# Up projection by seven block products, feed-forward weights in 512-column slots, down results added to the output by DMA

## What is computed

```python
u = rmsnorm(x) ; proj = u @ w_in          # 88 column tiles of 128
y_a = stick_breaking_attention(...)       # 8 heads x 128
y_b = hgrn2_chunkwise(...)                # 8 heads, rmsnorm, silu gate
m = sigmoid(gate_a) * (y_a @ p_a) + sigmoid(gate_b) * (y_b @ p_b)
h = x + m @ w_o
up = rmsnorm(h) @ w_up                    # 2048 -> 2 * 5632
up = causal_depthwise_conv(up, conv_w, conv_b)      # width 3, over tokens
gate, val = split(up)
out = h + (silu(gate) * val) @ w_down     # 5632 -> 2048
```

## Time and profile before

| | us |
|---|---|
| median of 3 runs | 2946.11 |
| lowest, highest | 2946.01, 2946.46 |
| span of the profiled execution | 2944.1 |

### The profile page before, as it was taken

The page is one execution under the profiler, slowest core; times in us unless marked ns, Lnnn a source line. Parts: engine busy times, 40 slices in busy tenths (PEclk is TensorE's granted clock), DMA queues, the critical chain, the costliest instruction groups (busy, mean ns, idle before and its releaser), DMA issues.

```text
span 2944.1 us, 35516 instructions
## 1 busy us (share of the span) xinstructions
PE 2918.1 (99%) x13156; PEld 2411.8 (82%) x13156; DVE 1423.5 (48%) x1931; ACT 887.3 (30%) x1064; POOL 70.4 (2%) x109
## 2 busy tenths in 40 slices
PE   7999999999999999999999999999999999999999
PEld 5888888888888888888888888888888888888887
DVE  7544454545455455444444445444444444444443
ACT  4332323232323233332233322223232222222231
POOL 3000000000000000001000000000000000000000
PEclk9999999999999999999999999999999999999999
DMA  4222222222232223444443332322322332333232
GB/s 160 83 96 83 98 84 96 90 90 90 89 98 83 94 85 122 145 139 144 143 171 101 95 98 97 98 99 95 98 97 95 99 97 97 98 96 100 93 101 100
DMA packets 82664, 304.35 MB, mean 103 GB/s; under 512 B 9632, under 2 KB 9632, under 8 KB 82384
## 3 DMA queue, kind: packets, MB, share of 16 engines
q1 hardware_dynamic: 74880, 272.66, 28.2%
q0 software_dynamic: 7632, 29.57, 2.9%
HBM read 285.42 MB, written 16.78 MB: 103 GB/s over the span
## 4 chain that ended last, share of the span: by engine, by line
PE 98%; DVE 2%; DMA 0%; ACT 0%; issue 0%; DVEq 0%; ACTq 0%; POOLq 0%
PE bank L1028 31%; PE bank L1030 31%; PE bank L1029 31%; PE bank L1074 2%; PE bank L1061 1%; PE bank L1119 1%; PE bank L1105 1%; DVE u_lo L620 1%; DVE w_lo L593 0%; PE bank L1134 0%; PE bank L1055 0%; PE bank L1050 0%; PE bank L1051 0%; DMA par<-params 0%; PE bank L1141 0%; PE bank L1142 0%
## 5 line engine op out<-in xcount | busy, mean ns | idle before, releaser
L593 DVE TENSOR_TENSOR w_lo<-w_raw,w_hi 128x1024 fp32r<-128x1024 f32 x504 | 620.5, 1232 | 727.5 <-ACT w_hi L373 710.2
L373 ACT ACTIVATE w_hi<-w_raw 128x1024 fp32r<-128x1024 f32 x504 | 529.6, 1051 | 640.0 <-PE bank L1030 639.2
L1028 PE MATMUL bank<-u_hi,w_hi 128*128 128x512 f32 x1408 | 557.4, 396 | 20.3 <-DVE u_lo L620 20.3
L1030 PE MATMUL bank<-u_hi,w_lo 128*128 128x512 f32 x1408 | 550.9, 391 | 0.0
L1029 PE MATMUL bank<-u_lo,w_hi 128*128 128x512 f32 x1408 | 550.4, 391 | 0.0
L1028 PE MATMUL bank<-v_hi,w_hi 128*128 128x512 f32 x1408 | 548.1, 389 | 0.0
L1030 PE MATMUL bank<-v_hi,w_lo 128*128 128x512 f32 x1408 | 547.7, 389 | 0.0
L1029 PE MATMUL bank<-v_lo,w_hi 128*128 128x512 f32 x1408 | 547.7, 389 | 0.0
L1028 PEld LDWEIGHTS bank<-u_hi,w_hi 128*128 128x128 f32 x1408 | 265.8, 189 | 76.1 <-issue 16.7
L1030 PEld LDWEIGHTS bank<-u_hi,w_lo 128*128 128x128 f32 x1408 | 265.4, 189 | 56.9
L1029 PEld LDWEIGHTS bank<-u_lo,w_hi 128*128 128x128 f32 x1408 | 266.0, 189 | 53.9 <-issue 0.2
(11 more groups left out here) (188 smaller groups left out, 2377.9 us busy)
## 6 DMA issues: line engine op xcount, KB each, us to landing
w_raw<-wstream SPq DMA_DIRECT2D x504, 512.0 KB, 3.3
gates_scratch<-g_out POOLq DMA_DIRECT2D x32, 256.0 KB, 2.9
g_in<-gates_scratch POOLq DMA_DIRECT2D x16, 512.0 KB, 4.0
x_in<-x_t SPq DMA_DIRECT2D x8, 512.0 KB, 9.0
xr<-x_t POOLq DMA_DIRECT2D x16, 256.0 KB, 3.2
h_scratch<-hb POOLq DMA_DIRECT2D x16, 256.0 KB, 2.3
h_acc<-h_scratch POOLq DMA_DIRECT2D x1, 4096.0 KB, 13.2
out_t<-h_acc SPq DMA_DIRECT2D x8, 512.0 KB, 2.6
```

Of the source, the lines that this page charges most:

```text
L373: act.activation(w_hi[:, slot * UC:(slot + 1) * UC], w_raw[:, slot * UC:(slot + 1) * UC], ACT.Copy).then_inc(w_hi_ready, 1)
L593: dve.tensor_tensor(w_lo[:, slot * UC:(slot + 1) * UC], w_raw[:, slot * UC:(slot + 1) * UC], w_hi[:, slot * UC:(slot + 1) * UC].bitcast(F3 ...
L1028: nc.tensor.matmul(out, wh, hi, start=first, stop=False)
L1030: return nc.tensor.matmul(out, wl, hi, start=False, stop=last)
```

## The change

The up projection takes blocks of two by two: the input channels in pairs of tiles (`KP` = 8 pairs), the tokens in halves of 256 (`HALF`), and gate and value tile as the two rows of a block matrix. Each product of two block matrices is computed as seven block products (`PRODUCTS`) in place of eight, with matmuls of 256 columns. For them:

- a slot of weights is [128, 512], four blocks for one tile and one pair; VectorE makes three more blocks from sums of them (`sums`), and a slot of 896 columns is split. A down slot is 512 columns, one output tile of a group. The slots stand in a ring of six, a load is released when TensorE is done with a slot (`slot_done`), sums are made three slots ahead and low parts two slots ahead;
- the normalised activation has three more blocks from sums (`t_sums`), made by VectorE in stage 3 and at the start of stage 4;
- PSUM holds the products in four banks; ScalarE copies the first (`p1_copy`), VectorE combines the rest (`combine`, `take_up`) and then multiplies with the token factor (`normalise`);
- four tiles (32 up slots) come before the loop; in the loop eight up slots of a tile are followed by four down slots; 16 down slots stand at the end.

Down results: ScalarE copies each from PSUM to one of two staging tiles, and GpSimd issues a transfer that adds it to the output in DRAM (`accum_op`), at most two at a time; h is written to the output directly, and `h_acc`, its reload and the final stores are gone.

In stages 1 to 3 the low part overwrites the raw weights, so that a load waits for `unit_done`, and `LEAD` is 2. The last four units of stage 3 are reordered, and its loop is unrolled for ScalarE and VectorE. The diff's core:

```diff
-LEAD = 3
+LEAD = 2
+PRODUCTS = [(A11, B11, 0, 0), (S2, T2, 0, 1), (A12, B21, 1, 0), (S4, B22, 1, 1),
+            (A22, T4, 2, 0), (S1, T1, 2, 1), (S3, T3, 3, 0)]
...
-                    sp_.wait_ge(w_ready, r * WSLOTS + (slot + 1 - WSLOTS))
+                    sp_.wait_ge(unit_done, r * WSLOTS + (slot + 1))
                     load_unit(r * WSLOTS + slot, slot)
...
+            for n in range(RING):
+                sp_.wait_ge(unit_done, WSLOTS + START4 - WSLOTS + min(n, WSLOTS - 1) + 1)
+                load_slot(n, n)
+            with sp_.Fori(0, SLOTS // RING - 1) as r:
+                for ring in range(RING):
+                    sp_.wait_ge(slot_done, r * RING + (ring + 1))
+                    load_slot(r * RING + (RING + ring), ring)
...
-            pool.dma_start(h_acc[:, :], h_dram).then_inc(h_back, 16)
+            pool.sem_inc(stage_free, 2)
+            for d in range(GROUPS * KT):
+                c = d % KT
+                pool.wait_ge(down_out, GROUP + d + 1)
+                pool.dma_start(out_t[:, c * SEQ:(c + 1) * SEQ], stage[d % 2][:, :],
+                               accum_op=ALU.add).then_inc(added[d % 2], 16)
+                if d > 0:
+                    pool.wait_ge(added[(d - 1) % 2], 16 * ((d - 1) // 2 + 1))
+                    pool.sem_inc(stage_free, 1)
...
+            def take_down(i, c):
...
+                act.wait_ge(slot_done, i * BODY + (FIRST + c + 1))
+                act.wait_ge(stage_free, d + 1)
+                act.activation(stage[j][:, :], bank[b][:, :], ACT.Copy).then_inc(down_out, 1)
...
+            def sums(i, c):
...
+                dve.wait_ge(w4_in[ring], loads * 16)
+                dve.tensor_tensor(blocks(w, S1, 2).rearrange("p (a c) -> p a c", a=2),
+                                  blocks(w, 0).unsqueeze(1).broadcast_to((P, 2, P)),
+                                  blocks(w, A22, 2).rearrange("p (a c) -> p a c", a=2),
+                                  ALU.add).then_inc(w4_step, 1)
+                dve.wait_ge(w4_step, u * 2 + 1)
+                dve.tensor_tensor(blocks(w, S2), blocks(w, S1), blocks(w, A11), ALU.add).then_inc(w4_step, 1)
+                dve.wait_ge(w4_step, u * 2 + 2)
+                dve.tensor_tensor(blocks(w, S4), blocks(w, A12), blocks(w, S2), ALU.add).then_inc(w4_sums, 1)
...
+            def lo_slot(i, c):
...
+                    dve.wait_ge(w4_hi_ready, n + 1)
+                    dve.tensor_tensor(w4_lo[ring][:, 0:width], w4_raw[ring][:, 0:width],
+                                      w4_hi[ring][:, 0:width].bitcast(F32), ALU.subtract).then_inc(w4_ready, 1)
...
+            def body4(i):
+                for c in range(BODY):
+                    fl, q = divmod(c, CYCLE)
+                    sums(i, c + 3)
+                    lo_slot(i, c + 2)
+                    if q < 2:
+                        conv_tap(i, fl - 1, 0, 1 - q)
+                    if 2 <= q < 4:
+                        conv_tap(i, fl - 1, 1, 3 - q)
+                    if q == 5:
+                        product(i, fl - 1)
+                    if q == 7:
+                        s_low(i, fl - 1)
+                    if q == KP:
+                        combine(i, fl)
...
+                    else:
+                        if q == KP + 1:
+                            take_up(i, fl)
+                        if q == KP + 2:
+                            normalise(i, fl)
...
+            def up_slot(i, c, kp, b0):
...
+                pe.wait_ge(w4_ready, n + 1)
+                for w, x, b, half in PRODUCTS:
+                    out = bank[b0 + b][:, half * HALF:(half + 1) * HALF]
...
+                    nc.tensor.matmul(out, wh, xh, start=kp == 0 and half == 0, stop=False, skip_group_check=True)
+                    nc.tensor.matmul(out, wh, xl_, start=False, stop=False, skip_group_check=True)
+                    ins = nc.tensor.matmul(out, wl, xh, start=False, stop=kp == KP - 1, skip_group_check=True)
+                ins.then_inc(slot_done, 1)
...
+            def down_slot(i, c, b, parity, d):
...
+                pe.wait_ge(down_out, d + 1)
+                pe.wait_ge(w4_ready, n + 1)
```

More of the change, by code:

```diff
@@ new lines, in _ @@
+            for i in range(KP - 1):
+                for p in range(4):
+                    split_ahead(START3, i, 4, p)
+                    if p == 0 and 0 < i < 6:
+                        hi_kp(i - 1)
+                    if p % 2 == 1:
+                        tile3(2 * i + p // 2)
+            split_ahead(START3, KP - 1, 4, 0)
+            split_ahead(START3, KP - 1, 4, 1)
+            act.wait_ge(unit_done, WSLOTS + START4 - 2)
+            hi_kp(5)
+            hi_slot(0, -FIRST)
+            hi_kp(6)
@@ L587, in _ @@
+            with act.Fori(0, BODIES - 1) as i:
+                body4(i)
+            body4(BODIES - 1)
+            for c in range(BODY, BODY + KT):
+                hi_slot(BODIES - 1, c + 3)
+                take_down(BODIES - 1, c - 1)
+            take_down(BODIES - 1, BODY + KT - 1)
         @block.vector
@@ new lines, in lo_slot @@
+            def lo_slot(i, c):
+                if exists(i, c):
+                    n, ring, loads, up = slot(i, c)
+                    width = WC if up else SC
+                    dve.wait_ge(w4_hi_ready, n + 1)
+                    dve.tensor_tensor(w4_lo[ring][:, 0:width], w4_raw[ring][:, 0:width],
+                                      w4_hi[ring][:, 0:width].bitcast(F32), ALU.subtract).then_inc(w4_ready, 1)
+            for i in range(KP - 1):
+                for p in range(4):
+                    split_ahead(START3, i, 4, p)
+                    if p % 2 == 1:
+                        tile3(2 * i + p // 2)
+                    if p == 1 and 0 < i < 6:
+                        lo_kp(i - 1)
+                    if p == 3 and i < 6:
+                        t_sums(i)
@@ L1020, in _ @@
+            with dve.Fori(0, BODIES - 1) as i:
+                body4(i)
+            body4(BODIES - 1)
+            for c in range(BODY, BODY + KT):
+                lo_slot(BODIES - 1, c + 2)
         @block.tensor
@@ L1162, in _, with unit3 @@
                         unit(i * 4 + (START2 + p), p, BANKS2[p], y_hi, y_lo, UK * br, True, True, y_ready, GROUP)
[L1165 to L1166 removed]
+            def unit3(i, p, c, half):
+                if half == 0:
                     pe.wait_ge(tile_out, i * 2 + (TILES3 + c + 1))
[L1168 to L1171 removed]
@@ new lines, in down_slot @@
+            def down_slot(i, c, b, parity, d):
+                n, ring, loads, up = slot(i, c)
+                pe.wait_ge(down_out, d + 1)
+                pe.wait_ge(w4_ready, n + 1)
+                for kk in range(GROUP):
+                    wh, wl = (t[ring][:, kk * P:(kk + 1) * P] for t in (w4_hi, w4_lo))
+                    sh, sl = s_hi[parity * GROUP + kk][:, :], s_lo[parity * GROUP + kk][:, :]
+                    nc.tensor.matmul(bank[b][:, :], wh, sh, start=kk == 0, stop=False)
+                    nc.tensor.matmul(bank[b][:, :], wh, sl, start=False, stop=False)
+                    ins = nc.tensor.matmul(bank[b][:, :], wl, sh, start=False, stop=kk == GROUP - 1)
+                ins.then_inc(slot_done, 1)
@@ L1209, in column_tiles @@
+            with pe.Fori(0, BODIES - 1) as i:
+                body4(i)
+            body4(BODIES - 1)
+            pe.wait_ge(s_ready, FT)
+            for c in range(KT):
+                down_slot(BODIES - 1, BODY + c, GROUP + c % 4, (GROUPS - 1) % 2, (GROUPS - 1) * KT + c)
 def column_tiles(w):
```

667 lines of the change are left out of this document (415 added, 252 removed).

## The result

The changed kernel takes 2919.1 us (2918.24 to 2919.46) where the kernel before takes 2946.24 beside it: a ratio of 0.9908, 95% interval 0.9894 to 0.9922. That is 27 us faster; the forecast was 74 us faster.

What follows compares the result with a forecast made beforehand. TensorE's matmul stream was taken as the bound, with VectorE as thinning cover. Terms -107.4 + 23 + 5 + 2 + 3 = -74 us took the median of 2946.1 to 2872 us; 8-in-10 range 2850 to 2932.

Steps and rivals of the forecast that it cites:

- term 1: Up projection: 7392 matmuls of 256 columns at 0.115 us replace 4224 of 512 at 0.2267, a gain of 107.4 us.
- term 2: Feed-forward loop: VectorE's 27.4 us per tile stays under TensorE's 30.2, so no stall; 0 us, bounds 0 to 60.
- term 3: First 32 up slots, without down slots: VectorE needs 23.4 us per tile against TensorE's 19.3, a loss of 23 us.
- term 4: Kernel start: unit 2's low part comes after the whole preparation, TensorE waits and restarts; 5 us lost, bounds 0 to 8.
- term 5: Kernel end: ScalarE copy and adding transfer cost 2 us, shared staging tiles with the last tile's chain 3, bounds 0 to 10.
- The cover: Loop: VectorE finishes before TensorE needs slot 6 of the next tile, at 24.2 against 25.4 us, 1.2 us left.
- VectorE as the loop's bound: Rival, 20%: slightly longer VectorE instructions use up the loop's 1.2 us and TensorE stalls every tile; 2905 to 2960 us.
- The slower rival: Rival, 12%: adding transfers land late and hold ScalarE's staging copies in the loop; 2987 us at 8 us landing.
- the third: Rival, 8% together with blocks not paying at all: weight load paces short matmuls at 0.125 us; 2941 us.

Runs made afterwards that it cites:

- e1: A kernel of its own with only long rows of back-to-back matmuls of one shape, a weight load at each; 256 fp32r columns take 120.0 ns.
- e2: Changed kernel with one addition in place of three dependent weight sums in the first 35 up slots; 2905.07 us, ratio 0.986.
- e6: Changed kernel with unit 2's split back in the preparation at the start; 2916.38 us, ratio 0.9899.
- e3: Changed kernel with the down results stored by plain transfers in place of adding ones; 2912.43 us, ratio 0.9884.
- e10: Changed kernel with unit 2's split back in the preparation and the last 16 down results added by VectorE, stored by the sync engine; 2901.10 us, ratio 0.985.

## Why the prediction was right and wrong

By its own steps, on the spans (forecast, measured):

| | forecast | measured |
|---|---|---|
| term 1, matmuls | -107.4 | -70.5 |
| term 2, stalls in the loop | 0 | +2.7 |
| term 3, first slots | +23 | +25.2 |
| term 4, start | +5 | +4.3 |
| term 5, end | +2 +3 | +10.2 |
| sum | -74 | -28.1 |

The spans differ by 27.9; the rest is rounding.

**The failed step is the size of term 1: "I take 0.115, from the row of the same shape".** The mechanism was right (TensorE at 100% in the loop, short matmuls at nearly half the price of long ones), the distance was not: 0.120, at the upper end of the bounds. It makes 37 of the 46 us that the sum missed by. Rows 6 are three matmuls, read to 10 ns, and e1 shows that a short row starts at 116 to 119 ns and settles at 120. The number stood elsewhere in the same profile: 0.2267 for 512 columns is 213.3 ns of columns at 2.4 GHz and 13.4 more. The lower bound, half of 0.2267, halves that fixed part too, which nothing allowed; 106.7 + 13.4 = 120.1 is what the row gives when it is taken apart. That this comes out so exactly is in part luck: in e1's own rows the part above the columns is 18.8 at 512 and 13.3 at 256, and the same working would give 125.5. With 0.120 the prediction's own sum would have been 2905, the upper end that it named; the other 14 us are terms 2, 3 and 5.

The Trainium skill (TensorE: Matmul & The Clock Gate, Back-to-back issue gap), with 262 cycles or an estimated 109 ns for 256 columns as what it calls the isolated gap, agrees with the bf16 rows of e1 (109.2) and not with fp32r, 120.0 in e1 and in the kernel. Its LDWEIGHTS rule of 107 ns for 128 columns is near the floor of 111.7 and, as quoted in the prediction, spoke against narrower blocks; e1 agrees, 192 and 128 columns cost the same.

**Term 2 held.** 27.4 us of VectorE per tile was forecast against 30.2 of TensorE. Measured, a tile takes 31.1 between the stops and VectorE waits 3.7 of it for the copy, so 27.4. The cover was forecast at slot 6 of a tile: 1.2 us, and 1.8 with 0.120. In the trace that slot's low part is ready 2.75 us before TensorE begins the slot (the median of the tiles). The 2.7 us are three short stops of 0.3 to 1.6 us between the loop's bodies, the largest in the chain in order of time:

```profile
2110.09 1.46 issue
2111.55 0.38 PE bank L1469
```

No engine's wait is named there. VectorE stops at the same place, for longer, and ScalarE too:

```profile
2112.55 0.43 DVE L1114 TENSOR_TENSOR w_raw<-w_raw 128x256 f32<-128x256 f32 x1 [3.74 <-issue]
```

VectorE's stop nearly uses up the cover: 15 us behind the first of these borders, at 1876.47, TensorE finds a low part that was ready for 0.06 us. The forecast of no stall was closer to failing than its result shows. What the engines stop for wasn't tried.

**Term 3 held in mechanism, e2 shows it**, but with 0.120 the same working gave 19 and not 23, so its size is 6 short. Of the 25.2, 16.3 are TensorE's idle time by the profile; a part of the rest is the clock. TensorE's rows after one of its waits for a low part:

```profile
1539.43 0.39 PE L1469 MATMUL bank<-v_hi,w_hi 128*128 128x256 f32 x1 [2.20 <-DVE w_lo L1128]
1539.65 0.28 PE L1470 MATMUL bank<-v_lo,w_hi 128*128 128x256 f32 x1
...
1540.93 0.41 PE L1471 MATMUL bank<-v_hi,w_lo 128*128 128x256 f32 x1
1541.14 0.41 PE L1469 MATMUL bank<-v_hi,w_hi 128*128 128x256 f32 x1
```

```profile
1530.00:1555.00 25.00, 22.40 (x169) 21.76 (x168) 22.75 (x44) 14.73 (x17) 0.00 (x0) 0.93 0.30 86
```

After 2.20 us of idle time the matmuls go on at 0.12 for 1.3 us and then stand 0.21 apart: the lower level, 1.2 GHz. In this stretch the granted clock is 0.93. After the longest wait, 4.08 us before 1616.32, the matmuls stand 0.21 apart at once and until 1619.05. The 16 and 13 matmuls of the two spells cost 2.7 us more than at 0.120. And after a short wait, as at 1539.43 above, the second start is 0.22 behind the first. A wait here costs more than its length, and the forecast had charged a restart at the start only.

**Term 4 held** (4.3 for 5), with its cause: the preparation ends at 39.9 where 40.2 was estimated, and e6 gives the time back.

**Term 5 is short by 5.** Landing was the open price, bounded 2.3 to 4.0 "nothing waits" and 5 "0.4 us per slot". It is 4.5, so the copies fall behind, and that with the longer landing is the 5.6 of e3. That a drain of GpSimd can stand at the end of the span was not in the sum. It is the other 5: e10, which has neither, ends as the kernel before.

**The rivals.** VectorE as the loop's bound didn't come: no wait for low parts after 1618 us. The slower rival needed landings of 5.9 us; the median is 4.5. Its sign, staging copies that wait for GpSimd, did show, 0.6 us per tile, and TensorE's loop has none of its stalls. For the third, 0.125 us, the truth is between it and the forecast: 0.120, and e1 says what it confuses: the weight load is the pace only up to 192 columns, at 111.7, and at 256 columns its width still adds to the distance.

The Trainium skill (SBUF — State Buffer, Who interferes with whom), by which a two-port instruction of VectorE delays the descriptors of GpSimd's transfers, would have fed the slower rival. The same section says that `tensor_tensor` has no two-port mode, and most of VectorE's work in this loop is that instruction, so it is no reason for a delay here. The runs agree: in the loop of e3 VectorE is at 83% and the plain stores land in 2.4 us, where h's landed in 2.3 at 43%. The h stores of the changed kernel take 3.3 us with VectorE at 46%, so the landing doesn't follow VectorE's load.

## What to carry to other kernels

Take a matmul's distance apart before it is scaled: columns over the clock, and a rest that isn't halved with the columns; here the rest alone decided between 107 and 70 us. How the rest goes with the shape must be measured (13.3 to 18.8 ns in e1), in a long row of that shape: three instructions are no price for seven thousand. And ask what each engine still has to do behind its last transfer, since an engine that was out of the way may now end the program.

## What the runs showed of the hardware

- fp32r matmuls with 128 weight columns, the weights changed each time: columns/2.4 + 13.3 ns from 256 to 320 columns, 16.0 above the columns at 384, 18.8 at 512 (13.4 in the kernels), and 111.7 at both 192 and 128. With 64 weight columns 229.3 at 512, 113.3 at 256 and 60.0 at 128. bf16 has 2.5 above the columns, at 256 as at 512.
- A GpSimd transfer of 256 KB that adds to DRAM lands in 4.5 us (median) and takes about 1.8 us of all 16 DMA engines; a plain one 2.4 and 0.7.
- A kernel in which GpSimd issued its last transfers near the end closes with a GpSimd drain of 5.05 to 6.7 us, whether they add or not. It lasts 5.05 to 5.3 when it begins behind the last landing.
- After an idle stretch of 2.20 us TensorE fell to the lower clock 1.3 us after it had started again, not at the restart; after one of 4.08 us it stood at the lower clock from the first matmul, for 2.7 us.
- At the borders of the changed kernel's loop VectorE stands idle for 3.3 to 3.7 us and TensorE for up to 1.5 us, with no wait named.
